# Attention scores from products of 128 rows, and probabilities multiplied by their inverse sums ahead of the turn

## The reference

```python
def dilated_branch(q, k, v, window, dilation, slopes):
    ...
    s = jnp.where(mask[None, None], s + bias[None, :, None], -jnp.inf)
    m = jnp.max(s, axis=-1, keepdims=True)
    p = jnp.exp(s - m)
    l = jnp.sum(p, axis=-1, keepdims=True)
    o = jnp.einsum('ghnqk,ghnkd->ghnqd', (p / l).astype(v.dtype), vb)
    ...
def dilated_mixture(q, k, v, slopes):
    ...
    alpha = jax.nn.softmax(jnp.stack(lses, 0), axis=0)
    out = jnp.sum(alpha[..., None] * jnp.stack(outs, 0), axis=0)
    ...
def sparse_attention(q_idx, k_idx, w_idx, q_lat, c_kv, slopes):
    ...
        _, idx = lax.top_k(score, topk)
        c_sel = jax.vmap(lambda cb, ib: cb[ib])(c_kv, idx)
        s = jnp.einsum('bqhr,bqkr->bhqk', ql, c_sel).astype(jnp.float32) * (HEAD_DIM ** -0.5)
        ...
        p = jax.nn.softmax(s, axis=-1)
        return jnp.einsum('bhqk,bqkr->bqhr', p.astype(c_sel.dtype), c_sel)
```

## Time and profile before

| | us |
|---|---|
| median of 3 runs (3891.0 to 3894.65) | 3894.07 |
| profiled execution, its own time | 3891.9 |
| its span, first to last instruction | 3890.1 |
| attention phase within the span | 2579.4 to 3020.5 |
| TensorE busy | 3525.0 (91%) |
| VectorE busy | 1913.2 (49%) |
| ScalarE busy | 1094.5 (28%) |
| GpSimd busy | 560.7 (14%) |
| mean granted clock of TensorE, in shares of full speed | 0.944 |

### The profile page before, as it was taken

How to read it: one execution, slowest core, us unless ns; L and a number is a source line. 1 busy time by engine, 2 the same in 40 slices (tenths; PEclk the granted TensorE clock), 3 DMA queues, 4 the chain that set the end, 5 groups by cost and what they waited for, 6 DMA issues and landing times. The chain is left out here.

```text
span 3890.1 us, 39586 instructions
## 1 busy us (share of the span) xinstructions
PE 3525.0 (91%) x15200; PEld 2739.0 (70%) x15200; DVE 1913.2 (49%) x2838; ACT 1094.5 (28%) x1710; POOL 560.7 (14%) x393
## 2 busy tenths in 40 slices
PE   7999788889788898999999998888889889999998
PEld 5776567657577586888888767755455768888886
DVE  4325444567441434555544549679666332424244
ACT  3222333233331222221112441134455221111112
POOL 0003364620100001100001200000045210000000
PEclk8999899889899999999999999988899989999999
DMA  3132332310231013322222202022111311111111
GB/s 115 71 101 83 112 116 76 119 62 1 95 87 60 12 49 108 109 92 97 93 86 76 76 11 60 30 58 54 41 25 28 119 38 44 54 43 54 43 54 54
DMA packets 221268, 263.18 MB, mean 68 GB/s; under 512 B 16827, under 2 KB 149844, under 8 KB 219074
## 3 DMA queue, kind: packets, MB, share of 16 engines
q1 hardware_dynamic: 221124, 261.22, 21.2%
HBM read 218.89 MB, written 29.18 MB: 64 GB/s over the span
## 5 line engine op out<-in xcount | busy, mean ns | idle before, releaser
L192 PE MATMUL psum<-rounded,rounded 128*128 128x512 f32 (+2 forms) x3936 | 1547.5, 393 | 181.3 <-POOL rounded L935 35.7
L193 PE MATMUL psum<-rounded,rounded 128*128 128x512 f32 (+2 forms) x3936 | 1537.3, 391 | 0.0
L194 PE MATMUL psum<-rounded,rounded 128*128 128x512 f32 (+2 forms) x3936 | 1536.3, 390 | 0.0
L192 PEld LDWEIGHTS psum<-rounded,rounded 128*128 128x128 f32 x3936 | 752.2, 191 | 359.3 <-POOL rounded L935 37.8
L194 PEld LDWEIGHTS psum<-rounded,rounded 128*128 128x128 f32 x3936 | 750.9, 191 | 153.2
L193 PEld LDWEIGHTS psum<-rounded,rounded 128*128 128x128 f32 x3936 | 752.1, 191 | 149.7 <-issue 0.2
L2714 DVE TENSOR_TENSOR plain<-psum,plain 128x512 f32<-128x512 f32 x432 | 288.6, 688 | 111.8 <-PE psum L194 110.1
L2725 DVE TENSOR_TENSOR plain<-psum,plain 128x512 f32<-128x512 f32 x44 | 30.4, 692 | 438.5 <-ACT plain L2634 438.5
L3091 DVE TENSOR_SCALAR_CACHE_REDUCE plain<-plain,plain 128x384 bf16<-128x384 f32 (+2 forms) x204 | 181.9, 942 | 1.3
L2706 DVE TENSOR_TENSOR rounded<-plain,rounded 128x512 fp32r<-128x512 f32 x108 | 96.4, 892 | 173.8 <-ACT rounded L2623 173.7
L3230 PE MATMUL psum<-plain,plain 128*128 128x512 f32 (+3 forms) x384 | 168.3, 551 | 0.9 <-ACT plain L3346 0.9
(11 more groups left out here) (299 smaller groups left out, 3595.0 us busy)
## 6 DMA issues: line engine op xcount, KB each, us to landing
plain<-in_ff_w_dram SPq DMA_DIRECT2D x64, 512.0 KB, 5.5
plain<-in_w_ada_dram SPq DMA_DIRECT2D x96, 256.0 KB, 3.3
plain<-in_w_gu_dram SPq DMA_DIRECT2D x44, 512.0 KB, 4.9
plain<-in_w_in_dram SPq DMA_DIRECT2D x36, 512.0 KB, 3.8
plain<-in_c_fwd_dram SPq DMA_DIRECT2D x64, 256.0 KB, 2.6
rounded<-rounded SPq DMA_DIRECT2D x48, 256.0 KB, 3.3
plain<-in_w_down_dram SPq DMA_DIRECT2D x22, 512.0 KB, 3.6
fold<-plain SPq DMA_DIRECT2D x8, 1024.0 KB, 4.7
```

The source lines that it names most:

```text
L192: nc.tensor.matmul(out, wh, xh, start=first, stop=False)
L193: nc.tensor.matmul(out, wh, xl, start=False, stop=False)
L194: return nc.tensor.matmul(out, wl, xh, start=False, stop=last)
```

## The change

The second score product takes 128 rows too: the query's low part, stacked twice, over the key's high and low part. `Stacks` has six tiles for a pair in place of four, and three more transfers.

The sums of the probabilities come from the exponential itself (`accum_out`), one value for a row. VectorE takes the reciprocal of these 128x1 (`scaled`), and the probabilities are multiplied by it in place ahead of the turn: on GpSimd in the dense heads, on VectorE in the sparse ones. Turns wait for this product (`row_ready`) instead of the exponential. The columns of ones, the reciprocals of 64x512 and the product of 64x512 go; `high` and `low` read PSUM, 64 rows at a time, for each head. Tiles move to other places in memory. The sparse heads' values are made a step earlier, the transfer of the value weights `w_uv_2` moves to the attention phase, ahead of the first bias, and the gate of the output product is loaded in two pieces, one of them again at the start of `phase_rows_gemm_norm`.

```diff
@@ -2847,63 +2849,56 @@
-        q0, q1, k0, k1 = (part.bitcast(F32) for part in self.sets[p % 2])
+        q0, q1, l0, l1, k0, k1 = (part.bitcast(F32) for part in self.sets[p % 2])
         sp.wait_ge(S["pair_hi"].sem, S["pair_hi"].at(2 * p + 1))
         sp.dma_start(q1[64:P, :], q0[64:P, :]).then_inc(S["odd_copied"].sem, 16)
         sp.dma_start(q1[0:64, :], q0[64:P, :]).then_inc(S["odd_copied"].sem, 16)
         sp.wait_ge(S["pair_hi"].sem, S["pair_hi"].at(2 * p + 2))
         sp.dma_start(k1[64:P, :], k0[64:P, :]).then_inc(S["odd_copied"].sem, 16)
+        sp.wait_ge(S["pair_lo"].sem, S["pair_lo"].at(2 * p + 1))
+        sp.dma_start(l1[64:P, :], l0[64:P, :]).then_inc(S["odd_copied"].sem, 16)
+        sp.dma_start(l1[0:64, :], l0[64:P, :]).then_inc(S["odd_copied"].sem, 16)
         sp.wait_ge(S["pair_lo"].sem, S["pair_lo"].at(2 * p + 2))
         sp.dma_start(k1[0:64, :], low[64:P, :]).then_inc(S["odd_copied"].sem, 16)
 
-        sp.wait_ge(S["odd_copied"].sem, S["odd_copied"].at(64 * (p + 1)))
+        sp.wait_ge(S["odd_copied"].sem, S["odd_copied"].at(96 * (p + 1)))
         sp.dma_start(q0[64:P, :], q0[0:64, :]).then_inc(S["even_copied"].sem, 16)
+        sp.dma_start(l0[64:P, :], l0[0:64, :]).then_inc(S["even_copied"].sem, 16)
         sp.dma_start(k0[64:P, :], low[0:64, :]).then_inc(S["even_copied"].sem, 16)
...
         nc, S, p, e = self.core.nc, self.core.sig, h // 2, h % 2
         if i == 0 and e == 0:
-            pe.wait_ge(S["even_copied"].sem, S["even_copied"].at(32 * (p + 1)))
-        rows, tile = slice(64 * e, 64 * e + 64), slice(i * P, (i + 1) * P)
-        q, k, low = self.sets[p % 2][e], self.sets[p % 2][2 + e], self.mixt.hi[:, p, :]
-        w = (i + 1) * P
+            pe.wait_ge(S["even_copied"].sem, S["even_copied"].at(48 * (p + 1)))
+        q, low, k = (self.sets[p % 2][2 * part + e] for part in range(3))
+        w, tile = (i + 1) * P, slice(i * P, (i + 1) * P)
         for a in range(0, w, BANK):
             b = min(a + BANK, w)
             out = self.core.psum[:, bank + a // BANK, 0:b - a]
             nc.tensor.matmul(out, q[:, tile], k[:, a:b], start=True, stop=False)
-            last = nc.tensor.matmul(out, low[rows, tile], k[rows, a:b], start=False, stop=True)
+            last = nc.tensor.matmul(out, low[:, tile], k[:, a:b], start=False, stop=True)
...
@@ -3179,6 +3168,7 @@
+            sp.dma_start(wuv.rearrange("p (h d) -> p h d", d=HD), ap["w_uv_2"][0].rearrange("h r d -> r h d")).then_inc(S["wuv_loaded"].sem, 16)
             bias(0)
             bias(1)
@@ -3205,7 +3195,7 @@
             def turns(n):
                 h, i = steps[n]
-                pe.wait_ge(S["act_done"].sem, S["act_done"].at(n + 1))
+                pe.wait_ge(S["row_ready"].sem, S["row_ready"].at(n + 1))
                 if n >= 1:
 
                     pe.wait_ge(S["probs_turned"].sem, S["probs_turned"].at(n))
@@ -3221,10 +3211,10 @@
                     pe.wait_ge(S["probs_turned"].sem, S["probs_turned"].at(ends[m] + 1))
                     if m >= 2:
 
-                        pe.wait_ge(S["row_ready"].sem, S["row_ready"].at(m - 1))
+                        pe.wait_ge(S["ft_lo"].sem, S["ft_lo"].at(m - 1))
                     if m == 2 * DENSE:
                         pe.wait_ge(S["act_free"].sem, S["act_free"].at(TT))
-                column = 192 * (h % DENSE // 2) + 64 * (h % 2)
+                column = P * (h % DENSE // 2)
@@ -3250,29 +3240,40 @@
-                    if 1 <= n - ends[m] <= 4:
+                    if 1 <= n - ends[m] <= 4 and not (m == 2 * DENSE - 1 and n == FIRST + 3):
                         values(m, n - ends[m] - 1)
-                if n == FIRST + 3:
+                if n == FIRST + 2:
+                    values(2 * DENSE - 1, 3)
                     sparse_values()
...
-            pool.wait_ge(S["chosen"].sem, S["chosen"].at(1))
-            for n in range(FIRST, N):
+            def bounded(n):
                 h, i = steps[n]
                 pool.wait_ge(S["x_ready"].sem, S["x_ready"].at(h - DENSE + 1))
...
-                if n == FIRST + 5:
+                if n == FIRST + 4:
                     pool.wait_ge(S["aux2_done"].sem, S["aux2_done"].at(TT))
                 if n >= FIRST + 2:
 
                     pool.wait_ge(S["dve_done"].sem, S["dve_done"].at(n - 1))
                 w = (i + 1) * P
                 nc.gpsimd.tensor_tensor(masked(n)[:, 0:w], biases[h % 2][:, L - w:L], sel_tile(core, i), ALU.add).then_inc(S["pool_done"].sem, 1)
+
+            for n in range(FIRST):
+                if n == FIRST - 2:
+                    pool.wait_ge(S["chosen"].sem, S["chosen"].at(1))
+                    bounded(FIRST)
+                    bounded(FIRST + 1)
+                w, one = (steps[n][1] + 1) * P, slice(n % 16, n % 16 + 1)
+                pool.wait_ge(S["dve_chain"].sem, S["dve_chain"].at(n + 1))
+                nc.gpsimd.tensor_scalar(probs[n % 2][:, 0:w], probs[n % 2][:, 0:w], total[:, one], None, ALU.mult).then_inc(S["row_ready"].sem, 1)
+            for n in range(FIRST + 2, N):
+                bounded(n)
@@ -3290,39 +3291,34 @@
                 nc.vector.tensor_tensor_reduce(out=probs[n % 2][:, 0:w], in0=pair(n, w), in1=b, scale=-SCALE, scalar=3.0e38,
-                                               op0=ALU.add, op1=ALU.min, accum_out=stat[:, n % 16:n % 16 + 1]).then_inc(S["dve_done"].sem, 1)
-
-            def divided(m):
+                                               op0=ALU.add, op1=ALU.min, accum_out=least[:, n % 16:n % 16 + 1]).then_inc(S["dve_done"].sem, 1)
+
+            def scaled(n):
+                h, i = steps[n]
+                w, one = (i + 1) * P, slice(n % 16, n % 16 + 1)
+                dve.wait_ge(S["act_done"].sem, S["act_done"].at(n + 1))
+                nc.vector.reciprocal(total[:, one], total[:, one]).then_inc(S["dve_chain"].sem, 1)
+                dve.wait_ge(S["dve_chain"].sem, S["dve_chain"].at(n + 1))
+                if h >= DENSE:
+                    nc.vector.tensor_scalar(probs[n % 2][:, 0:w], probs[n % 2][:, 0:w], total[:, one], None, ALU.mult).then_inc(S["row_ready"].sem, 1)
+
+            def low(m):
                 h, b = m // 2, m % 2
-                rows, sums = slice(64 * (h % 2), 64 * (h % 2) + 64), slice(64 - 64 * (h % 2), P - 64 * (h % 2))
-                dve.wait_ge(S["aux_done"].sem, S["aux_done"].at(m + 1))
-                if m >= 1:
-
-                    dve.wait_ge(S["row_ready"].sem, S["row_ready"].at(m))
-                nc.vector.reciprocal(inverse[rows, :], ps[sums, 6 + m % 2, :]).then_inc(S["dve_chain"].sem, 1)
-                dve.wait_ge(S["dve_chain"].sem, S["dve_chain"].at(m + 1))
-                nc.vector.tensor_tensor(mixt.raw[rows, h // 2, b * BANK:(b + 1) * BANK], ps[rows, 6 + m % 2, :], inverse[rows, :], ALU.mult).then_inc(S["row_ready"].sem, 1)
-
-            def low(m):
-                p, b = m // 4, m % 2
-                cols = slice(b * BANK, (b + 1) * BANK)
-                dve.wait_ge(S["ft_hi"].sem, S["ft_hi"].at(2 * p + b + 1))
-                nc.vector.tensor_tensor(mixt.lo[:, p, cols], mixt.raw[:, p, cols], mixt.hi_raw[:, p, cols], ALU.subtract).then_inc(S["ft_lo"].sem, 1)
+                rows, cols = slice(64 * (h % 2), 64 * (h % 2) + 64), slice(b * BANK, (b + 1) * BANK)
+                dve.wait_ge(S["ft_hi"].sem, S["ft_hi"].at(m + 1))
+                nc.vector.tensor_tensor(mixt.lo[rows, h // 2, cols], ps[rows, 6 + m % 2, :], mixt.hi_raw[rows, h // 2, cols], ALU.subtract).then_inc(S["ft_lo"].sem, 1)
 
             biased(0)
-            for n in range(N + 6):
+            for n in range(N + 5):
                 if n + 1 < N:
                     biased(n + 1)
                 if n < N:
                     h, i = steps[n]
                     if h % 2 == 0 and h // 2 + 1 < HEADS // 2 and i in (4, 5):
                         stacks.low(dve, h // 2 + 1, i - 4)
-                if n - 2 in finished_at and finished_at[n - 2] // 2 % 2 == 1:
-                    low(finished_at[n - 2])
+                    scaled(n)
                 if n in finished_at:
-                    divided(finished_at[n])
-                if n == N + 5:
-                    low(blocks - 1)
+                    low(finished_at[n])
                 if n < CHOSEN_BY:
@@ -3332,7 +3328,8 @@
                 act.wait_ge(S["dve_done"].sem, S["dve_done"].at(n + 1))
-                nc.scalar.activation(probs[n % 2][:, 0:w], probs[n % 2][:, 0:w], ACT.Exp, scale=-1.0, bias=stat[:, n % 16:n % 16 + 1]).then_inc(S["act_done"].sem, 1)
+                one = slice(n % 16, n % 16 + 1)
+                nc.scalar.activation(probs[n % 2][:, 0:w], probs[n % 2][:, 0:w], ACT.Exp, scale=-1.0, bias=least[:, one], accum_out=total[:, one]).then_inc(S["act_done"].sem, 1)
@@ -3358,16 +3355,15 @@
             def high(m):
-                p, b = m // 4, m % 2
-                cols = slice(b * BANK, (b + 1) * BANK)
-                act.wait_ge(S["row_ready"].sem, S["row_ready"].at(m + 1))
```

(10 more changed lines are left out.)

71 lines of the change are left out of this document (30 added, 41 removed).

## The result

The changed kernel takes 4070.64 us, median of 4 runs (4063.7 to 4079.65), against 3894.11 us for the kernel before: 1.0456 times the time, 95% interval 1.0432 to 1.048. The forecast was 4120 us (3985 to 4205), slower. The profiled execution took 4066.42 us, 174.5 more than that of before; its attention phase lasts from 2579.4 to about 3195.5 us, 616 instead of 441 us, which is the whole difference.

What follows compares the result with a forecast made beforehand. The prediction took a non-overlapping chain through TensorE, VectorE and GpSimd as the bound: eight dense heads plus 13 us (289), eight sparse (362), sparse values 10, tail 9, giving 670 us against 441, hence 4120 us (3985 to 4205).

Steps and rivals of the forecast that it cites:

- The closed chain: Attention steps: turns n, scores and addition n+2, reciprocal, multiplication and turns n+1 follow without overlap; dense head 30.6 us, sparse 40.7.
- GpSimd's product: Dense heads: multiplying probabilities on GpSimd costs 4.6 us per head, priced like a store with one stream in, one out.
- the upper bound that I had set: Dense heads: GpSimd's product costs at most its two-input addition, 12.2 us per head.
- Score products: TensorE, every head: 128 rows instead of 64 cost nothing; score products stay at 8.9 us per head.
- The wait for GpSimd: Sparse heads: VectorE's product waits for GpSimd's addition, putting 12.2 us of additions and 4.1 of products into the chain.
- The one-off terms and the tail: Attention phase outside the head times: 13 us in dense heads, 10 for sparse values, 9 for the tail.
- The clock: TensorE at the low level 0.3 of dense and 0.4 of sparse time: heads 34.5 and 45.3 us.
- the dear GpSimd product: Rival, dense heads: GpSimd's product costs as much as its addition, 7.6 us more per head, 4180 us; chance 0.11.
- the clock and the missing wait: Two rivals: clock stays up with the wait, 4054 us, chance 0.12; no wait for GpSimd, 4026 us, chance 0.20.
- The rival on the other side: Faster: VectorE loses 129 us of work, dense heads fall to 23.3 us, total 3861 us; chance 0.04.

Runs made afterwards that it cites:

- the swap: Changed kernel with VectorE's reciprocal of step n (in sparse heads also its product) moved ahead of the addition of step n+1: 3883.99 us, ratio 0.9977.
- the later addition: Changed kernel with GpSimd's addition for step n in sparse heads also waiting for VectorE's product of step n-3: 3993.21 us, ratio 1.025.
- the form with an accumulator: Changed kernel with VectorE's product in the sparse heads also writing its row's sum into an unneeded column: 4013.1 us, ratio 1.0298.
- an edit of the second product alone: Kernel before with the second score product reading 128 rows like the first, the query's low part left out: 3871.66 us, ratio 0.9943.
- the slower score products: Changed kernel with the second score product over 64 rows again, leaving out the product of the two low parts: 4173.39 us, ratio 1.072.

## Why the prediction was right, and where its sizes were off

The closed chain is shown: it stands in the rows of the changed kernel, and the swap alone removes 187 us while GpSimd's price stays (1.73 us) and VectorE's falls only in part (0.97). The wait of VectorE's product for GpSimd is shown by two edits that touch nothing else, the later addition (1649 to 589 ns) and the form with an accumulator (813 ns). By the Trainium skill (SBUF — State Buffer, "Who interferes with whom") a `tensor_scalar` in a two-port mode can grab the pair of ports shared with GpSimd, but not the form that also writes out its accumulator; these runs agree, with 1649 and 813 ns. The same section says that whoever issues first keeps the pair. In the records VectorE's product starts 0.03 us before GpSimd's addition (3089.11 and 3089.14, 3116.11 and 3116.14) and still waits it out, so either the starts in the records are not the moment that decides or the rule isn't the whole of it; no run here tells.

The size came out 50 us too high through terms that went opposite ways; that they left so little is luck.

- **GpSimd's product, taken as 4.6 us per dense head: 14.5.** It lies above the upper bound that I had set, 12.2. The step that failed is the choice "one stream in, one out, nearest to the store", and the bound itself: an operation with one tile and a column of factors cost more than one with two tiles. In the groups by width of the changed kernel it takes 605 ns at 128 columns and 2943 at 1024, about 2.6 ns a column. The Trainium skill's figure (GPSIMD Engine Reference, 3.1: 1.03 cycles per element, at 1.2 GHz) would give 0.88 us for 1024 columns as an estimate; the measurement decides. VectorE isn't the reason: the product of 1024 columns at 2850.80 took 2.84 us with VectorE idle. Why it is so dear was not tried.
- **Score products, taken as free of their height: 8.9 us per head for TensorE, now 4.7.** That is six pairs of 0.31 + 0.23 at 512 columns, and 0.12, 0.06 and 0.18 for each of four at 256, 128 and 384. The step that failed read "0.32 us with 64 rows against 0.33 with 128" as the cost of each height. These were products in alternation, and the alternation is what costs: taking it away by an edit of the second product alone also moved the first one's spacing from 0.40 to 0.32 us (the second's went from 0.43 to 0.23). I compared two products that share the condition I should have varied. The row to compare with stood in the trace of before, whose large products (lines 192 to 194) are of 128 rows throughout and start 0.23 us apart:

```profile
298.30 0.40 PE L194 MATMUL psum<-rounded,rounded 128*128 128x512 f32 x1
298.53 0.40 PE L192 MATMUL psum<-rounded,rounded 128*128 128x512 f32 x1
...
3000.94 0.47 PE L2886 MATMUL psum<-rounded,rounded 128*128 128x512 f32 x1
3001.34 0.50 PE L2887 MATMUL psum<-rounded,rounded 64*128 64x512 f32 x1
3001.77 0.49 PE L2886 MATMUL psum<-rounded,rounded 128*128 128x512 f32 x1
```

Could 64 rows be dear by themselves? Plain products of 64 rows that follow one another (line 668, 512 columns) start 0.43 us apart, and plain ones of 128 rows (line 3230) as well; from the last of 64 rows to the next product of 128 it is 0.52 (297.21 to 297.73). That speaks for the alternation; rounded products of 64 rows in a row occur in no run here, so it isn't shown for them. It was worth 4.2 us of chain per head, and 103 us in this kernel with what the clock added.
- **The wait for GpSimd, taken as 12.2 + 4.1 us per sparse head: 13.2.** The reading was right that the product stands until the addition ends, but 0.2 us of its own time are over by then, and in some steps the addition starts 1.1 us ahead of it. 3.1 us too much.
- **The one-off terms and the tail, 32 us: about 18.** By 616 - 8 x 39.3 - 8 x 35.5. The tail is 8.7 us (3186.8 to 3195.5), as the sum had 9. The other 9, for which I had 23, lie in the head at the change from dense to sparse, which takes 49.0 us: there the addition waits 8.3 us for GpSimd, and GpSimd 17.5 us for the sparse values (L3232 in the groups). What the selection and the splits stick out in the dense heads is inside the 39.3.
- **The clock.** The handling was right in kind. With the measured terms a dense head is 5.1 + 4.7 + 6.1 + 1.3 + 14.5 + 3.2 + 0.4 + 1.2 = 36.5 us at full clock and 46.3 at the low one; the row's 0.75, half the time low, makes 40.8, against 39.3 measured. A sparse head is 34.8 and 44.6, and with 0.82 makes 37.8, against 35.5. I had assumed 0.3 and 0.4 of the time at the low level; by the rows it was 0.5 and 0.36. Which of the terms holds the 1.5 and 2.3 us that the sums are still too high isn't separated.

So dense heads were predicted at 34.5 and measured at 39.3 (38 us too low for eight), sparse ones at 45.3 and 35.5 (78 too high), and the rest 14 too high: together 54 us in the phase. Of the rivals, the dear GpSimd product was true as well (by more than its 7.6 us), the clock and the missing wait were not. The rival on the other side had named its point: product, reciprocal and handovers must fit in 0.3 us per step, or the orders must overlap. The swap is that overlap, and it turned the sign.

## What to carry to other kernels

Follow one item through every engine's order before pricing anything: when step n+1's result sits behind step n+2's work on one engine, and that work behind step n's on another, all prices in the ring add up, and exchanging two neighbours can be worth more than any of them. A price read from a trace holds under the conditions of that trace; look for what its rows have in common (here a change of height between neighbours) before saying what it depends on. For an instruction that no row shows, a bound from a "heavier" instruction is a guess, not a bound: GpSimd's product cost more than its two-input addition. And when an order is changed to spare one instruction a wait, look at what now stands in its place: here the split took back 7.9 us.

## What the runs showed of the hardware that I had not expected

- TensorE: products of rounded f32 tiles with 128 rows, one behind the other, start 0.23 us apart at 512 columns (0.31 for the first pair behind the turns); in alternation with 64 rows 0.40 and 0.43. Moving one side to 64 rows lengthened the mean of both (487 to 583 and 428 to 594 ns, part of it the lower clock).
- GpSimd: product with a column of factors 0.61 us at 128 and 2.94 at 1024 columns on average, against 0.77 and 2.66 for the sum of two tiles.
- VectorE: the plain product waits until GpSimd is done although its record starts 0.03 us earlier; with an accumulator output it doesn't, 0.81 against 1.65 us. The split, with two tiles in, waits as well (2.36 to 2.71 instead of 1.22 us).
- The clock went with the chain: the same TensorE work ran at 0.75 and 0.82 in the changed kernel and at 0.88 and 0.99 with two instructions exchanged; with the slower score products it was 0.64 and 0.63.
